# GpSimd's high parts as tensor_scalar with constants, and its split loops written out

## The reference

```python
# first block
proj = rms_norm(h, g_mix_pre) @ w_in          # pooled part u, and q, k, v
...                                           # pool mixer; stick-breaking attention
h = h + rms_norm(mix, g_mix_post)             # mix = concat(...) @ w_out
m = rms_norm(h, g_mlp_pre) @ w_up
m = jnp.square(jax.nn.relu(m)) @ w_down
h = h + rms_norm(m, g_mlp_post)
gate = jax.nn.sigmoid(h @ w_ple_gate)
h = h + gate * rms_norm(p @ w_ple_proj, g_ple)
# second block: modulated norm, w_in_2, two attentions (MLA and a forgetting one),
# two output projections, w_out_2, then a convolved and gated MLP (w_up_2, w_down_2)
```

## Time and profile before

| | |
|---|---|
| median of three runs | 3059.92 us |
| the profiled execution | 3058.98 us |
| its span, first to last instruction | 3057.2 us |
| TensorE (PE) busy | 2947.8 us, 96% |
| TensorE weight loads (PEld) | 2343.9 us, 77% |
| VectorE (DVE) busy | 1590.9 us, 52% |
| ScalarE (ACT) busy | 793.6 us, 26% |
| GpSimd (POOL) busy | 1059.4 us, 35%, 469 instructions |
| mean granted TensorE clock | 0.984 |

### The profile page before, as it was taken

One profiled execution on the slowest core, in us unless ns is written; L12 is line 12 of the kernel. 1 busy time (PEld: TensorE's weight loads), 2 busy tenths in 40 slices (PEclk: granted clock), 3 DMA queues, 4 the chain that ended last, 5 costly groups with the idle time before them and its releaser, 6 DMA issues.

```text
span 3057.2 us, 34071 instructions
## 1 busy us (share of the span) xinstructions
PE 2947.8 (96%) x13230; PEld 2343.9 (77%) x13230; DVE 1590.9 (52%) x1574; ACT 793.6 (26%) x1067; POOL 1059.4 (35%) x469
## 2 busy tenths in 40 slices
PE   6999998899999999899999999999999999999997
PEld 5876666688888888678888866766887888888886
DVE  3629964635655465884332165555546333343356
ACT  2128953311222121331002133234003111111112
POOL 2330023244444444254444430410453333333342
PEclk9999999999999999999999989999999999999999
DMA  2120032112222222131323344421421111111112
GB/s 109 49 75 17 13 117 90 35 62 103 96 96 93 99 96 69 69 133 46 113 71 125 109 92 127 107 49 33 160 96 35 49 48 48 48 48 48 49 48 75
DMA packets 85010, 233.02 MB, mean 76 GB/s; under 512 B 19312, under 2 KB 27760, under 8 KB 84144
## 3 DMA queue, kind: packets, MB, share of 16 engines
q1 hardware_dynamic: 79616, 211.49, 21.0%
q10 hardware_dynamic: 5296, 20.19, 1.7%
HBM read 176.26 MB, written 28.05 MB: 67 GB/s over the span
## 4 chain that ended last, share of the span: by engine, by line
PE 73%; issue 8%; DVE 7%; POOL 2%; ACT 1%; SPq 0%; DMA 0%; POOLq 0%; DVEq 0%; ACTq 0%
PE ps L416 55%; PE ps L470 4%; PE ps L1296 3%; PE ps L2439 2%; PE ps L2412 2%; PE ps L2116 1%; PE ps L2453 1%; DVE stick_sp L1044 1%; PE ps L2829 1%; POOL w_hi L316 1%; POOL w_lo L319 1%; DVE stick_sp_hi L1055 1%; DVE stick_a L1068 1%; PE ps L3323 1%; DVE stat L2528 0%
## 5 line engine op out<-in xcount | busy, mean ns | idle before, releaser
L316 POOL TENSOR_TENSOR w_hi<-w_raw,inv_count 128x1024 fp32r<-128x1024 f32 x186 | 357.8, 1924 | 1537.3 <-PE ps L416 960.0
L319 POOL TENSOR_TENSOR w_lo<-w_raw,w_hi 128x1024 fp32r<-128x1024 f32 x186 | 494.2, 2657 | 14.6
L416 PE MATMUL ps<-x_hi,w_hi 128*128 128x512 f32 x1104 | 342.3, 391 | 6.1 <-DVE qkvu_raw L893 4.8
L416 PE MATMUL ps<-x_lo,w_hi 128*128 128x512 f32 x1104 | 340.9, 390 | 0.0
L416 PE MATMUL ps<-x_hi,w_lo 128*128 128x512 f32 x1104 | 340.7, 390 | 0.0
L416 PEld LDWEIGHTS ps<-x_hi,w_hi 128*128 128x128 f32 x1104 | 207.6, 188 | 51.3 <-issue 6.5
L416 PE MATMUL ps<-hidden_hi,w_hi 128*128 128x512 f32 x800 | 246.3, 389 | 0.0
L416 PE MATMUL ps<-hidden_lo,w_hi 128*128 128x512 f32 x800 | 246.3, 389 | 0.0
L416 PE MATMUL ps<-hidden_hi,w_lo 128*128 128x512 f32 x800 | 246.3, 389 | 0.0
L416 PEld LDWEIGHTS ps<-x_lo,w_hi 128*128 128x128 f32 x1104 | 207.8, 188 | 43.5
L416 PEld LDWEIGHTS ps<-x_hi,w_lo 128*128 128x128 f32 x1104 | 207.8, 188 | 43.4
(11 more groups left out here) (448 smaller groups left out, 5267.9 us busy)
## 6 DMA issues: line engine op xcount, KB each, us to landing
w_raw<-wall SPq DMA_DIRECT2D x213, 512.0 KB, 3.2
ada_raw<-wada SPq DMA_DIRECT2D x48, 512.0 KB, 4.2
gates_scratch<-gate_out ACTq DMA_DIRECT2D x16, 512.0 KB, 2.6
gate_in<-gates_scratch SPq DMA_DIRECT2D x8, 1024.0 KB, 8.3
residual<-x_t SPq DMA_DIRECT2D x8, 512.0 KB, 8.7
residual<-x_t SPq DMA_DIRECT2D x2, 2048.0 KB, 9.4
emb_scratch<-emb_out ACTq DMA_DIRECT2D x8, 512.0 KB, 2.6
embedding<-emb_scratch SPq DMA_DIRECT2D x4, 1024.0 KB, 6.4
```

Source lines behind the costliest of these rows:

```text
L316: nc.gpsimd.tensor_tensor(w_hi[:, slot, :], w_raw[:, slot, :], one.to_broadcast([P, S]), ALU.mult).then_inc(w_split, 1)
L319: nc.gpsimd.tensor_tensor(w_lo[:, slot, :], w_raw[:, slot, :], w_hi[:, slot, :].bitcast(F32), ALU.subtract).then_inc(w_split, 1)
L416: last = nc.tensor.matmul(ps[:, banks + c, :], lhs, x[:, k0 + k, c * HALF:(c + 1) * HALF], start=k == 0 and n == 0, stop=k == nk - 1 and n ...
```

## The change

In six places the high part becomes a `tensor_scalar` that multiplies by two constants 1.0 in the instruction; the result is the same. And `split_blocks` no longer loops: its blocks are written out one by one. The line numbers of the changed kernel are lower by up to 12 behind these places.

```diff
--- before.py
+++ after.py
@@ -313,18 +313,10 @@
         def split(b, slot, landed):
             pool.wait_ge(w_landed[slot], landed)
             pool.wait_ge(w_used, b + 1)
-            nc.gpsimd.tensor_tensor(w_hi[:, slot, :], w_raw[:, slot, :], one.to_broadcast([P, S]),
-                                    ALU.mult).then_inc(w_split, 1)
+            nc.gpsimd.tensor_scalar(w_hi[:, slot, :], w_raw[:, slot, :], 1.0, 1.0, ALU.mult, ALU.mult).then_inc(w_split, 1)
             pool.wait_ge(w_split, b * 2 + 1)
             nc.gpsimd.tensor_tensor(w_lo[:, slot, :], w_raw[:, slot, :],
                                     w_hi[:, slot, :].bitcast(F32), ALU.subtract).then_inc(w_split, 1)
-        pairs = (last - first) // 2
-        if pairs > 1:
-            with pool.Fori(0, pairs) as i:
-                for u in range(2):
-                    b = first + u
-                    split(i * 2 + b, b % 2, i * 16 + 16 * (b // 2 + 1))
-            first += 2 * pairs
         for b in range(first, last):
             split(b, b % 2, 16 * (b // 2 + 1))
 
@@ -346,7 +337,7 @@
         high, low = spare
         pool.wait_ge(w_landed[b % 2], 16 * (b // 2 + 1))
         pool.wait_ge(w_split, b * 2)
-        nc.gpsimd.tensor_tensor(high, raw, one.unsqueeze(2).to_broadcast([P, 2, HALF]), ALU.mult).then_inc(w_split, 1)
+        nc.gpsimd.tensor_scalar(high, raw, 1.0, 1.0, ALU.mult, ALU.mult).then_inc(w_split, 1)
         pool.wait_ge(w_split, b * 2 + 1)
         nc.gpsimd.tensor_tensor(low, raw, high.bitcast(F32), ALU.subtract).then_inc(w_split, 1)
 
@@ -394,8 +385,7 @@
         pool.wait_ge(*spare_in.at(32))
         for u in range(2):
             high, low = spares[u]
-            nc.gpsimd.tensor_tensor(high, raw[u], one.unsqueeze(2).to_broadcast([P, 2, HALF]), ALU.mult
-                                    ).then_inc(spare_split.sem, 1)
+            nc.gpsimd.tensor_scalar(high, raw[u], 1.0, 1.0, ALU.mult, ALU.mult).then_inc(spare_split.sem, 1)
             pool.wait_ge(*spare_split.at(2 * u + 1))
             nc.gpsimd.tensor_tensor(low, raw[u], high.bitcast(F32), ALU.subtract).then_inc(spare_split.sem, 1)
             pool.wait_ge(*spare_split.at(2 * u + 2))
@@ -2644,8 +2634,7 @@
             for t, raw in zip(later_split, (raw2[:, FQ + p, :], raw2[:, FK + p, :])):
                 if t is later_split[1]:
                     pool.wait_ge(*kq_split.at(4 * p + 2))
-                nc.gpsimd.tensor_tensor(t[:, 0, :], raw, one.to_broadcast([P, S]), ALU.mult
-                                        ).then_inc(kq_split.sem, 1)
+                nc.gpsimd.tensor_scalar(t[:, 0, :], raw, 1.0, 1.0, ALU.mult, ALU.mult).then_inc(kq_split.sem, 1)
                 pool.wait_ge(*kq_split.at(4 * p + (1 if t is later_split[0] else 3)))
                 nc.gpsimd.tensor_tensor(t[:, 1, :], raw, t[:, 0, :].bitcast(F32), ALU.subtract
                                         ).then_inc(kq_split.sem, 1)
@@ -2966,8 +2955,7 @@
                 pool.wait_ge(*moved[(p - 1) % 2][half].at(64 * ((p + 1) // 2) + (64 if half == 0 else 0)))
             pool.wait_ge(*set_rows.at(5))
             pool.wait_ge(*k_split.at(2 * p))
-            nc.gpsimd.tensor_tensor(km_hi[:, :], km[:, p, :], one.to_broadcast([P, S]), ALU.mult
-                                    ).then_inc(k_split.sem, 1)
+            nc.gpsimd.tensor_scalar(km_hi[:, :], km[:, p, :], 1.0, 1.0, ALU.mult, ALU.mult).then_inc(k_split.sem, 1)
             pool.wait_ge(*k_split.at(2 * p + 1))
             nc.gpsimd.tensor_tensor(km_lo[:, p, :], km[:, p, :], km_hi[:, :].bitcast(F32), ALU.subtract
                                     ).then_inc(k_split.sem, 1)
```

## The result

The changed kernel takes 3040.27 us (median of 4 runs, 3036.88 to 3041.57) beside 3059.61 us of the kernel before (4 runs in the same session): ratio 0.9933, 95% interval 0.9919 to 0.9947. The direction was right and the size was not: 19.3 us came, 12.4 were forecast, and the median lies 1.2 us under the range.

The account below looks back on a forecast made before the run. TensorE (PE) was taken to bound the kernel, so only its stops between stages counted. Terms summed to 12.45 us off 3058.98, giving 3046.5; with 0.94 to the median, 3047.5 us, range 3041.5 to 3054.

Parts of the forecast that it names:

- One high part: Cost of one GpSimd high part: 1.90 us falls to 1.05 alone; about 1.9 when it meets VectorE, bounds 1.25 and 2.75.
- Term 1: Gate stage, block GG+6: PE's 2.74 us stop and the slow clock behind it go; 4.8 us, bounds 2.7 and 5.8.
- Term 2: First output projection, two places: VectorE operation that PE awaits starts earlier behind a shorter high part; 1.7 us together.
- Term 3: Entry of the gate stage: VectorE's chain to PE shortens by 0.8 us near 1245.38 and 0.85 at 1281.77.
- Term 4: Entry of the second input projection: a VectorE operation waits for a low part that now ends earlier; 0.85 us.
- Term 5: Second output projection, next stage: PE waits for a GpSimd low part behind a high part; 0.85 us.
- Term 6: Both attentions and entry of the up projection: held VectorE operations before PE stops end earlier; 2.6 us, bounds 0 and 4.
- the two smaller places: Places near 1971 and 2312 us where held VectorE operations precede PE stops; 0.9 us together.
- the 9 that I forecast: Sign over the whole kernel: PE's idle time lower by 9 us, its busy time by about 3 from the clock.
- Term 7: Weight-block loops written out, 474 GpSimd rows instead of 206: worth nothing, covered by GpSimd's 6.50 us wait for PE.
- more clock comes back: Rival: slow clock behind PE's stops before 1287.6 and 1363.2 also goes, 1.7 us each; 3043 us, chance 0.15.
- The three others: Rivals: VectorE stays behind (3051 us, 0.12); change fails where it counts (3054.9, 0.08); GpSimd loses its turns (3069, 0.03).

Follow-up runs that it names:

- gate_four: Constants only in the four high parts of the gate stage's chain, loops written out, against the kernel before: 3054.81 us beside 3060.22, ratio 0.9987.
- fox_two: Constants only in two high parts (query, key) of the forgetting attention's second round, loops written out, against the kernel before: 3055.46 us beside 3060.22, ratio 0.9986.

## Why the prediction was wrong in size

- **One high part**: right. 1.05 us alone and 1.9 met, both as forecast.
- **Term 1, gate chain, 4.8 us**: 5.9 in three traces of the changed kernel; its four high parts alone give 5.4 (gate_four). VectorE keeps up with the statistic, which I had doubted; without the cheaper part of GG+7 it does not (1.36 us).
- **Term 2, 1.7**: 1.5. **Term 3, 0.8 + 0.85**: 0.8 and 0.8, the second with another 1.6 us of clock in two of three traces. **Term 4, 0.85**: 0.5 to 1.0. **Term 5, 0.85**: 0.7, and 0.3 just behind it.
- **Term 6, 2.6 with bounds 0 and 4**: this is the step that failed. Fox alone is 4.8 us (I had 0.7), mla alone 4.3 (I had 1.0); at the two smaller places (0.9) nothing shows beyond what differs between executions. Two things were wrong in it. For mla I priced one held VectorE operation, where two high parts in a row are met: 2 x 0.86 = 1.7 us of idle, 2.78 to 1.08. And for both I left the clock out, though I had counted it in term 1 and the earlier trace rows showed what follows a stop; I never asked for the windows behind the stops at 1788.44 and 2023.03. By PE's busy time in the windows above the lower clock there was worth 3.4 us in fox and 2.7 in mla. The whole trace says the same: PE's idle time fell by 9.3 us (109.4 to 100.1), the 9 that I forecast, and its busy time by 12.8 (2947.8 to 2935.0), where I had about 3. In the two other traces of the changed kernel idle fell by 11.6 and 10.9, busy time by 5.7 and 8.1.
- **Term 7, loops, 0**: -0.4 us by the medians, -3.1 to +2.4 by the interval.
- **The rivals**: "more clock comes back" was the right kind at the wrong places. At the two stops that it named the lower level stayed in the first trace; in the two others it was gone behind the first of them. The three others did not come.

Term by term the traces give 5.9 + 1.5 + 0.8 + 0.8 + 0.8 + 1.0 + 4.4 + 3.9 = 19.1 us (mla as the middle of 3.3 and 4.5, since before's own stretch differs by 1.2 us between executions), beside the measured 19.3. That the two agree so well is in part luck. The sum takes fox from the longer kind of execution (2.9 would do as well as 4.4) and leaves out the 1.6 us of term 3. It leaves out one place that got worse, too: between the matmuls of the MLP's entry the changed kernel took 81.3, 83.3 and 81.9 us in its three traces, where before took 79.9, with longer stretches at 1.2 GHz behind nearly the same stops. Whether the change brings that on or the execution is open; fox_two, whose code there is that of before, took 81.9.

## What to carry to other kernels

A stop of TensorE has two prices: its idle time, and up to half of whatever runs at the lower clock behind it, less where another engine is due next anyway. Read the window behind every stop that a change may remove, however short the stop is, and in more than one execution: 0.67 us stood for 2.9 to 4.4. And when an engine with time to spare gets faster, list the places where it meets a chain to the bound engine, count each instruction in a row there, and try the list alone: 19 of 206 instructions carried the whole gain.

## What the runs showed of the hardware

- GpSimd, 128x1024 f32, alone: two constants in the instruction 1.05 us, product with a broadcast column 1.90, product of a tile with itself 1.89, subtraction of two tiles 2.40, one column as the scalar operand 2.85.
- The last one lets VectorE pass (1.28 us at 429.68, as alone) and is itself stretched, to 7.48 us among half-tile operations. The product is stretched there too (5.65 us at 1382.71), but in the meetings of 1024 elements it holds VectorE up until it ends (1.96 us for 1.28 at 430.24).
- The same stops in the same code are followed by different stretches at 1.2 GHz from one execution to the next: the entry of the MLP took 79.90 us in before and 81.90 in fox_two, and 81.3 to 83.3 us in three traces of the changed kernel.
